# Routing the first token tile inside the merge stage, with reordered expert loads and value gathers woven between key gathers

## What is computed

```
q = (xb @ w_query).reshape(tn, PEER_HEADS, 2, PK_HALF)            # 8 heads, 2 halves of 128
s = einsum('thkd,hknd->thkn', q, sub_keys)                         # 128 keys for each half
top_s, top_i = top_k(s, 16)
cand_s = top_s[:, :, 0, :, None] + top_s[:, :, 1, None, :]         # 256 candidates
cand_i = top_i[:, :, 0, :, None] * N_KEYS + top_i[:, :, 1, None, :]
best_s, best_j = top_k(cand_s, 16)
experts = take_along_axis(cand_i, best_j)                          # 8*16 = 128 experts per token
act = gelu(einsum('thkd,td->thk', expert_u[experts], xb))
out = einsum('thk,thkd->td', softmax(best_s) * act, expert_v[experts])
x = LN2(alpha*x + out)
```

## Time and profile before

| what | us |
|---|---|
| median of 3 executions (5275.3 to 5281.16) | 5277.45 |
| the profiled execution, its time | 5260.49 |
| its span, first to last instruction | 5258.6 |
| VectorE busy in the span | 3327.4 (63%) |
| TensorE busy | 3984.0 (76%) |
| GpSimd busy | 1476.5 (28%) |

### The profile page before, as it was taken

How to read it: one execution, slowest core, us unless ns; L and a number is a source line. 1 busy time by engine, 2 the same in 40 slices (tenths; PEclk the granted TensorE clock), 3 DMA queues, 4 the chain that set the end, 5 groups by cost and what they waited for, 6 DMA issues and landing times. The chain is left out here.

```text
span 5258.6 us, 61057 instructions
## 1 busy us (share of the span) xinstructions
PE 3984.0 (76%) x24165; PEld 3204.5 (61%) x24165; DVE 3327.4 (63%) x4454; ACT 933.3 (18%) x1274; POOL 1476.5 (28%) x1641
## 2 busy tenths in 40 slices
PE   8999999999968887999998999999999700000000
PEld 7999999999955666997896555555555400000000
DVE  2323333343336666334445977879788799999998
ACT  2222232232222233223341000000000000000000
POOL 0000000000044441000010222222222377777774
PEclk9999999999978888999999999999999855555555
DMA  4332332333269996326566999999999999999998
GB/s 158 115 129 96 104 111 96 109 101 104 80 235 353 346 356 248 110 102 219 165 222 222 418 421 418 396 418 421 421 420 421 394 403 410 409 410 410 409 410 330
DMA packets 339992, 1462.12 MB, mean 278 GB/s; under 512 B 87268, under 2 KB 116356, under 8 KB 199928
## 3 DMA queue, kind: packets, MB, share of 16 engines
q0 software_dynamic: 175328, 995.65, 46.9%
q1 hardware_dynamic: 133608, 430.42, 22.9%
q10 hardware_dynamic: 30768, 32.11, 1.8%
HBM read 1362.71 MB, written 94.75 MB: 277 GB/s over the span
## 5 line engine op out<-in xcount | busy, mean ns | idle before, releaser
L2242 DVE SCALAR_TENSOR_TENSOR i_acc<-i_row,i_cf,i_acc 128x2048 f32<-128x2048 f32 x571 | 1344.8, 2355 | 156.7 <-DMA i_row<-in_expert_v,i_ei 120.4
L2049 PE MATMUL i_p_h<-i_xT,i_ut 128*128 128x384 f32 x4096 | 1322.0, 486 | 0.0
L2049 PEld LDWEIGHTS i_p_h<-i_xT,i_ut 128*128 128x128 f32 x4096 | 778.8, 190 | 540.8 <-DMA i_xT<-tmp_x1T 0.3
L2358 POOL DMA_INDIRECT i_row<-in_expert_v,i_ei x576 | 545.9, 948 | 635.5 <-DVE i_acc L2242 511.2
L265 PE MATMUL a_acc<-a_xh,a_wh 128*128 128x288 f32 x3104 | 672.4, 298 | 18.5 <-DVE a_xl L491 13.4
L265 PE MATMUL a_acc<-a_xh,a_wl 128*128 128x288 f32 x3104 | 665.6, 296 | 0.0
L265 PE MATMUL a_acc<-a_xl,a_wh 128*128 128x288 f32 x3104 | 665.0, 296 | 0.0
L265 PEld LDWEIGHTS a_acc<-a_xh,a_wh 128*128 128x128 f32 x3104 | 499.7, 189 | 30.0 <-issue 27.8
L2233 DVE CUSTOM_DVE_ANT_0 i_row<-i_row,i_acc 128x2048 f32<-128x2048 f32 x192 | 433.7, 2286 | 126.0 <-DMA i_row<-in_expert_u,i_ei 124.1
L265 PEld LDWEIGHTS a_acc<-a_xl,a_wh 128*128 128x128 f32 x3104 | 500.8, 189 | 0.0
L265 PEld LDWEIGHTS a_acc<-a_xh,a_wl 128*128 128x128 f32 x3104 | 500.8, 189 | 0.0
(11 more groups left out here) (314 smaller groups left out, 5337.8 us busy)
## 6 DMA issues: line engine op xcount, KB each, us to landing
i_ut<-in_u_tiles SPq DMA_DIRECT2D x128, 1024.0 KB, 9.6
a_w<-in_w_in SPq DMA_DIRECT2D x97, 1024.0 KB, 4.9
f_w<-in_w_out SPq DMA_DIRECT2D x32, 1024.0 KB, 5.1
f_w<-in_w_query SPq DMA_DIRECT2D x32, 1024.0 KB, 5.2
tmp_Ha<-i_ho ACTq DMA_DIRECT2D x128, 192.0 KB, 9.2
tmp_uT<-a_out POOLq DMA_DIRECT2D x65, 288.0 KB, 2.4
f_w<-in_w_bs SPq DMA_DIRECT2D x16, 1024.0 KB, 4.8
tmp_xcT<-f_cv POOLq DMA_DIRECT2D x32, 288.0 KB, 4.3
```

The costliest lines, as they stand in the source:

```text
L2049: last = nc.tensor.matmul(p_h[:, e % 2, 0:ND], ut[:, e % RU, k * P:(k + 1) * P], xT[:, k, :], start=(k == 0), stop=(k == KT - 1))
L2242: v.scalar_tensor_tensor(acc, row[:, m % R, :], cf[:, j, k:k + 1], acc, ALU.mult, ALU.add).then_inc(row_used, 1)
L2358: pool.indirect_dma_start(row[:, m % R, :], None, table, bass.IndirectOffsetOnAxis(index, axis=0)).then_inc(row_in[m % R], 16)
```

## The change

1. Tile 0 is scored and routed in the merge stage: its keys are loaded there (`f_sk`), TensorE makes the 16 products straight from `qo`, one behind each of the query items 2 to 17; ScalarE copies them in two halves at items 10 and 18; VectorE does the routing in 18 parts behind items 14 to 31 (`ROUTE_AT` of `front`). Expert numbers and gate scores stay in two new tiles of SBUF that live through the program, `r_ei0` and `r_gt0`.
2. In the expert stage the routing of tile 0 is gone. GpSimd's first gather waits for `i_xT` instead. SP's list starts with `i_ut` tile 0 and `i_xT`; then come `x1`, the queries of tile 4, the keys, `i_ut` tile 1 and the rest. The scores of tile 4 are made behind dense tile 3 (before: behind tile 7); `keys(2)` now stands ahead of tile 6 (before: after tile 15).
3. In the fused stage value pages 0 to 4 are gathered between key pages 6 to 15, one behind each odd key page. The semaphores of the pages are held through the program.

Cut to its core:

```diff
@@ mamba_and_samples, GpSimd
                     for c in range(RK, PAGES):
                         page_k(b, c)
-                    for c in range(8):
+                        if c % 2:
+                            page_v(b, c // 2 - RK // 2)
+                    for c in range(5, 8):
                         page_v(b, c)
@@ front
+        ROUTE_AT = {14: (0,), 16: (1,), 17: (2,), 18: (3,), 19: (4,), ...
+                def scores(m):
+                    pe.wait_ge(q_out, m + 1)
...
+                    nc.tensor.matmul(acc[:, 4 + m // 4 % 2, m % 4 * NK:(m % 4 + 1) * NK], qo[:, m % 4, 0:P], sk[:, m, :],
+                                     start=True, stop=True).then_inc(scored, 1)
...
                         query(i)
+                        if 2 <= i - Q1 < NTL + 2:
+                            scores(i - Q1 - 2)
...
+                    if i in (Q1 + 10, Q1 + 18):
+                        copy_scores((i - Q1 - 10) // 8)
...
+                    for part in ROUTE_AT.get(i - Q1, ()):
+                        route(part)
@@ peer
-    SCORES_AT = {1: 1, 2: 4, 3: 7, 4: 11}
-    GATE_AT = {0: 1, 1: 3, 2: 6, 3: 10, 4: 14}
-    ROUTE_AT = {0: 1, 11: 2, 21: 3, 33: 4}
-    GATES_AT = {6: 0, 8: 1, 19: 2, 30: 3, 43: 4}
+    SCORES_AT = {1: 0, 2: 4, 3: 7, 4: 11}
+    GATE_AT = {0: 0, 1: 3, 2: 6, 3: 10, 4: 14}
+    ROUTE_AT = {1: 1, 11: 2, 21: 3, 33: 4}
+    GATES_AT = {0: 0, 8: 1, 19: 2, 30: 3, 43: 4}
...
-                keys(1)
                 for half in range(2):
                     sp.dma_start(x1[half * TS:half * TS + TS, 1, :], dr["x1"][TP:T, :]).then_inc(x1_in[1], 16)
-                tiles(0, SCORES_AT[1] + 1)
                 keys(2)
-                tiles(SCORES_AT[1] + 1, SCORES_AT[2] + 1)
+                tiles(0, SCORES_AT[2] + 1)
...
+                dense(0, 4)
+                scores(1)
+                dense(4, 8 * SCORES_AT[2])
...
-                pool.wait_ge(routed, 1)
+                for q in range(4):
+                    pool.wait_ge(xT_in[q], 16)
                 for k in range(PICKS):
-                    gather(k, io["expert_u"], ei[:, 0, k:k + 1])
+                    gather(k, io["expert_u"], ei0[:, k:k + 1])
```

168 lines of the change are left out of this document (134 added, 34 removed).

## The result

| | median us | runs |
|---|---|---|
| before | 5276.38 | 4 (5274.31 to 5281.16) |
| after | 5335.07 | 4 (5327.15 to 5340.77) |

The ratio is 1.0107 with a 95% interval from 1.0091 to 1.0123; by the medians the change costs 58.7 us. The profiled execution of after took 5327.15 us (span 5325.5), the shortest of its four.

A forecast was written before the change was run, and what follows sets the result against it. Gathers and dense products were taken to reach the stores' wait together, the later bounding the expert stage. Expert +29, merge +4 and fused +9 made +42 us: 5302 by the profiled execution, 5320 against the median; range 5279 to 5350.

The forecast's parts named there:

- the likeliest case: Expert stage: dense tile 6 waits 22 to 32 us, the rest as forecast; 5305 to 5340 us, chance 0.66.
- The gathers' side: Expert stage: first gather 52 us sooner, reaching the wait for the stores with some 50 us of slack.
- The dense side, start: Expert stage head: dense tile 0 starts sooner, but u tile 1 comes later; +2 us, from -6 to +10.
- Tile 6: Expert stage: TensorE waits for u tile 6 behind the slow keys(2) queries load; 26 us, bounds 0 to 32.
- The clock: Dense products: TensorE runs at a lower clock after the pause; 4 us, from 0 to 5.
- Sum for the dense products: Expert stage: start 2, tile 6 26 and clock 4 together make +32 us.
- Expert stage: Whole stage: dense products' +32 us less 3 regained at the stores' wait; +29 us, from -7 to +45.
- Merge stage: Query projection: TensorE's 16 added products cost 4 us (2 to 8); VectorE's routing is hidden, cost 0.
- Fused stage: Page gathers: woven value pages make key page 15 some 2.2 us later; +9 us, from -15 to +25.
- the queries share by bytes: Expert stage rival: keys(2) queries share by bytes, tile 6 is in time; sum +12, 5289 us, chance 0.14.
- Weaving pays: Fused stage rival: value pages fill empty DMA time, gaining 12 us, stall kept; +21, 5298 us, chance 0.12.
- The gathers were the only chain: Expert stage rival: the stores' wait is no wait, 52 us reach the end; -39, 5238 us, chance 0.04.

The follow-up runs named there:

- e2: After with the load of tile 1's queries back behind u tile 15 in SP's list; 5300.45 us, ratio 1.0044.
- e4: After with GpSimd's first expert gather held until dense tile 4 is done, keys(2) still ahead of tile 6; 5299.49 us, ratio 1.0047.
- e3: After with the keys(2) load reading 1 MB of keys in 8 KB pieces instead of queries, at the same place; 5369.11 us, one run.
- e1: After without the weaving: value pages 0 to 7 gathered behind key page 15; 5315.39 us, ratio 1.0068.
- e9: e7 with u tiles 2 to 5 ahead of tile 4's queries and the keys, tile 4's scores behind dense tile 7; 5286.39 us, ratio 1.0031.
- e10: e9 with GpSimd's first gather held until two dense tiles are done; 5249.20 us, ratio 0.9959.
- e12: e10 once more, unchanged, in a later batch; 5257.78 us, ratio 0.9973.
- e5: After without weaving, with four small unused 64 KB gathers per group where value pages had been woven in; 5327.21 us, ratio 1.0097.
- e7: After unwoven, keys(2) late, u tile 1 ahead of tile 4's queries, x1, keys; tile 4's last 8 value gathers before the stores' wait; 5355.24 us, ratio 0.9994.
- e8: The kernel before with tile 4's last 8 value gathers moved ahead of the wait for the stores; 5368.77 us, ratio 1.0023.
- second batch: Follow-up runs, e3, e7 and e8 among them, on a chip of their own; the kernel before took 5357.55 us there.

## Why the prediction was right, and where not

The forecast was 5320 us in 5279 to 5350, slower; the result is 5335.07, slower, and the likeliest case is the one that came. The change costs 58.7 us where the sum had 42; 7 of the difference lie in the expert stage and 9.5 in the fused stage. (One slip in the working: the upper end takes 20 us for the fused stage, whose own bound is 25.) By its own steps:

- **The gathers' side** (52 us sooner, slack at the wait): the first gather went out 14.3 us after SP's first load, forecast 14.6. But GpSimd waited 52.8 us for the stores and not some 80: the gathers came to the wait 16.6 us sooner, not 50, and the pick 35.9 later. It cost nothing here, since the dense products decide. The step that failed is that a stream started 52 us sooner stays 52 us ahead: it ran beside a full set of transfer engines (415 GB/s), and I didn't ask how much transfer time stood empty in the head, which was 21 us.
- **The dense side, start** (+2, bounds -6 to +10): measured +6.9 at tile 1. I had u tile 1 land 26.6 us after SP's first load; it landed 31.4 after. It was issued at 15.8 us, since SP was held 9.42 us at the keys ahead of it, and took 15.6 us beside the first gathers. In those 15.6 us SP's queue moved 2.44 MB and GpSimd's 3.56 MB, where I had given SP half.
- **Tile 6** (26, bounds 0 to 32): measured 28.49, with the load at 44.2 us (forecast 40 to 44) and the u tile 4.9 us behind it (3 to 5). e2 takes the pause away by the load's place, e4 by the gathers, e3 by the size of its pieces. The mechanism holds in all its parts.
- **The clock** (4): after each pause the first 4 us run at 0.50, behind the long one the next 4 at 0.78. That makes 2 + 0.9 us for the long one and 1.9 for the short one, found as the rest between tiles 1 and 4: 4.8.
- **Sum for the dense products** (+32): 6.9 + 28.5 + 4.8 = 40.2, measured 39.4 at the last tile; 3.5 come back at the wait (forecast 3). **Expert stage +36.1, forecast +29**: the start is most of the difference.
- **Merge stage** (+4): +3.4, with VectorE's 48.7 us more hidden.
- **Fused stage** (+9, bounds -15 to +25): +18.5, the largest miss. I took the delay of key page 15, less a gap and slack on the page before it. The waits show more: 38 key waits for 22 in seven groups, so not page 15 alone came late. So late keys are right as the mechanism, but not their size. Of the 18.5, 9.2 us are time outside TensorE's busy time, which is the forecast's 9, and that match is partly luck: the waits for keys grew by 33.0, and other waits shrank. The other 9.3 are busy time at a lower granted clock, a term that the sum put at nothing; its cause stays open. The pair of traces alone gives +26.0, just outside the bound.
- **The profiled execution against the median** (17 us below): the offset was carried rightly, but most of it lies in the fused stage, 554.4 us for a mean of 563.9 over unwoven kernels.

Of the rivals, "the queries share by bytes" fell with the 44.2 us and e3. It leaned on the Trainium skill ("DMA: Bandwidth & Descriptors", Specifications: pieces of 512 bytes and more at full line rate); that two queues would then share by bytes was my reading of it. The traces don't contradict the sentence for a load without gathers beside it (512 KB in 4.1 us, 1 MB in 6.1 in e4). Beside gathers they do: SP's queue moved 1.07 MB in 42 us. "Weaving pays" fell with e1. "The gathers were the only chain" fell with the wait of 52.78 us.

## What to carry to other kernels

Where the transfers are full behind it, as here, an earlier start is worth no more than the transfer time that stood empty in the head; read the GB/s of that stretch before pricing the start. A load in small pieces took seven to eight times as long beside the gathers' large packets as without them (1 MB in 512-byte pieces: 44.2 to 51.4 us for 6.1), so put it where nothing else streams, or behind enough work, and hold the big stream back for a few us if need be: e9 and e10 differ only in 17 us of that, and by 0.7%. With the loads placed so, the weaving undone and the slack used, the change went from 1% slower to 0.3 to 0.4% faster (e10, e12). And when two streams take turns on one issuing engine, an extra turn ahead of the one that is waited for makes it late (42 waits for keys in e5, 20 in e1). Before you price such waits by the length of a stage, compare the granted clock of the two traces.

## What the hardware showed that I had not expected

- Half the bytes in half the piece size took longer still beside gathers: 512 KB in 256-byte pieces 75.5 us (e9), for 44.2 us of 1 MB in 512-byte pieces (after). The u tiles ahead of it in the queue are in the 75.5; in e10, with the same tiles ahead and the gathers held, it is 22.3.
- SP can be held at an issue itself: 49.32 us at the keys in e9, 17.20 in e10, 9.42 in after, each time right behind a load in small pieces. Every load behind it in the program is then late, even if it waits for nothing.
- A stream that started 59 us later made the whole some 32 us shorter (e4 against after, by the ratios; 31.5 in the expert stage).
- The fused stage's length follows TensorE's granted clock in it: unwoven, leaving the second batch's chip aside, it takes 554.4 and 556.7 us at 0.84 and 0.85, 564.8 at 0.83, and 568.3 to 570.1 at 0.81 to 0.82, with the same instructions.
- An issue order that costs nothing where it replaces idle time (e7, 9.0 us less) costs 11.2 us where there is none (e8), though it moves the same 8 gathers. Why e8 loses and doesn't come out even stays open: its first pick comes 23.4 us later, since the 8 gathers go out at the pace of VectorE's rows, and no run takes apart what follows.
